# Moving a norm's statistics, transposes and scaled rows ahead of the down projection in the context's first feed-forward

## The reference, cut to what matters

```python
x = first_block(...)                       # ends: x = x + moe(h); return rms_norm(x, final_norm_g)
# second block, layer 0; x_lat is x, x_ctx is the context, 256 tokens x 1024 features each
x_ctx = x_ctx + 0.5 * mc[2] * swiglu(modulate(x_ctx, g, mc[0], mc[1]), w_gate, w_up, w_down)
x_lat = x_lat + 0.5 * m[2]  * swiglu(modulate(x_lat, g, m[0],  m[1]),  w_gate, w_up, w_down)
# modulate(x, g, shift, scale) = x * rsqrt(mean(x*x) + eps) * g * (1 + scale) + shift
# swiglu(x) = (silu(x @ w_gate) * (x @ w_up)) @ w_down, with 2816 hidden features
```

## Time and profile before

| | us |
|---|---|
| median of 3 runs | 2166.23 |
| lowest, highest | 2163.4, 2167.1 |
| the profiled execution, its time | 2169.83 |
| its span, first to last instruction | 2168.0 |

### The profile page before, as it was taken

The page is one execution under the profiler, slowest core; times in us unless marked ns, Lnnn a source line. Parts: engine busy times, 40 slices in busy tenths (PEclk is TensorE's granted clock), DMA queues, the critical chain, the costliest instruction groups (busy, mean ns, idle before and its releaser), DMA issues. The chain is left out here.

```text
span 2168.0 us, 32219 instructions
## 1 busy us (share of the span) xinstructions
PE 2019.4 (93%) x13104; PEld 1613.9 (74%) x13104; DVE 1275.3 (59%) x2026; ACT 882.4 (41%) x1436; POOL 60.5 (3%) x72
## 2 busy tenths in 40 slices
PE   7999999989998889888799999999999999999998
PEld 7897887744445657667788878668888888888887
DVE  5877455462112333334587763577777777877776
ACT  4434354311001222224455443375445554545444
POOL 1000000000000000000100030000001000100000
PEclk9999999989999999999999999999999999999999
DMA  9999984469999999999346453034446464364441
GB/s 363 402 399 359 372 292 155 171 257 422 421 421 414 414 407 410 406 418 331 129 144 233 167 163 117 10 108 165 159 136 230 156 225 155 129 213 166 143 155 40
DMA packets 211166, 540.73 MB, mean 249 GB/s; under 512 B 8894, under 2 KB 105752, under 8 KB 186440
## 3 DMA queue, kind: packets, MB, share of 16 engines
q1 hardware_dynamic: 208264, 531.69, 65.1%
q0 software_dynamic: 2192, 6.57, 1.1%
q10 hardware_dynamic: 560, 0.38, 0.1%
HBM read 537.56 MB, written 1.05 MB: 248 GB/s over the span
## 5 line engine op out<-in xcount | busy, mean ns | idle before, releaser
L1305 PE MATMUL lo<-xs,wp 128*128 128x512 f32 (+1 forms) x3392 | 594.4, 337 | 11.6 <-DVE wp L2678 8.3
L1305 PEld LDWEIGHTS lo<-xs,wp 128*128 128x128 f32 x3392 | 515.8, 190 | 89.7 <-issue 12.8
L987 ACT ACTIVATE wp<-ring 128x1024 fp32r<-128x1024 f32 (+2 forms) x432 | 347.3, 828 | 252.4 <-PE hi L1305 142.0
L2678 DVE TENSOR_TENSOR wp<-ring,wp 128x1024 fp32r<-128x1024 f32 (+2 forms) x432 | 398.8, 943 | 12.0 <-ACT wp L987 11.9
L1305 PE MATMUL hi<-hs,wp 128*128 128x256 f32 (+1 forms) x1842 | 318.8, 334 | 6.3 <-DVE hs L3030 3.2
L1305 PEld LDWEIGHTS hi<-hs,wp 128*128 128x128 f32 x1842 | 276.6, 190 | 45.1 <-DVE hs L3030 3.5
L1305 PE MATMUL lo<-ring,scratch 128*64 128x512 f32 (+1 forms) x1536 | 253.4, 594 | 17.3 <-DMA ring<-in_moe_w_up_dram 9.3
L1305 PEld LDWEIGHTS lo<-ring,scratch 128*64 128x64 f32 (+1 forms) x1536 | 79.7, 123 | 176.7 <-issue 163.7
L2685 DVE TENSOR_TENSOR ring_r<-ring,home 128x1024 fp32r<-128x1024 f32 x52 | 63.0, 1224 | 133.4 <-ACT home L995 133.4
L995 ACT ACTIVATE home<-ring 128x1024 fp32r<-128x1024 f32 x52 | 53.9, 1053 | 189.9 <-DMA ring<-in_ffn_w_down_dram 57.8
L1305 PE MATMUL hi<-xs,home 128*128 128x256 f32 x576 | 108.3, 292 | 14.4 <-DVE ring_r L2685 12.0
(11 more groups left out here) (494 smaller groups left out, 2758.4 us busy)
## 6 DMA issues: line engine op xcount, KB each, us to landing
ring<-in_mod_w_dram SPq DMA_DIRECT2D x72, 1024.0 KB, 15.2
ring<-in_moe_w_gate_dram SPq DMA_DIRECT2D x64, 1024.0 KB, 12.4
ring<-in_moe_w_up_dram SPq DMA_DIRECT2D x64, 1024.0 KB, 15.9
ring<-in_moe_w_down_dram SPq DMA_DIRECT2D x64, 1024.0 KB, 15.4
ring<-in_ffn_w_gate_dram SPq DMA_DIRECT2D x55, 1024.0 KB, 6.0
ring<-in_ffn_w_up_dram SPq DMA_DIRECT2D x55, 1024.0 KB, 8.7
ring<-in_ffn_w_down_dram SPq DMA_DIRECT2D x50, 1024.0 KB, 11.0
ring<-in_w_in_dram SPq DMA_DIRECT2D x20, 1024.0 KB, 13.2
```

Source lines behind the costliest of these rows:

```text
L987: act.activation(wp[:, q % SLOTS, 0, k:k + w.shape[1], :], w, ACT.Copy).then_inc(piece_hi, 2 // len(parts))
L1305: return pe.matmul(dst, lhsT, rhs, start=start, stop=stop, **kw)
L2678: tt(wp[:, q % SLOTS, 1, k:k + w.shape[1], :], w, wp[:, q % SLOTS, 0, k:k + w.shape[1], :].bitcast(F32), ALU.subtract).then_inc(piece_lo, ...
```

## The change: what it does

The order of the steps is changed, and two banks with it; the same values are computed.

- Step 1 moves up on ScalarE: the first half goes behind the rounding of piece 53, the second behind the rounding of hidden tile 17. The roundings of pieces 54 and 55 are now behind both.
- Step 2 moves up on VectorE, now a reciprocal and a product for each half, between the product and the rest of hidden tile 17; the rest of piece 54 comes behind it.
- Step 3 moves from behind up tile 19 to behind up tile 18, and the copy and the square of step 4 from tile 20 to tile 18.
- Step 5 moves from behind up tile 21 to behind up tile 19, into bank hi 0 in place of lo 0. TensorE now waits for rms_std ahead of the down pieces.
- Step 6: the square root goes ahead of the silu of tile 20, the reciprocal to VectorE's tile 20.
- Step 7: chunks 0 to 3 are scaled at VectorE's tile 20, 4 to 7 at tile 21. ScalarE's shift of chunk d comes ahead of the square of the context's chunk d, and VectorE's rest follows one down piece later.

```diff
@@ ScalarE @@
             act.wait_ge(piece_done, EARLY_PIECES - 1)
             round_piece(EARLY_PIECES + 1)
+            act.wait_ge(moe_done, 1)
+            norm_stats(4, x, squares=part(10240, TT, D), halves=(0,))
             early_piece(EARLY_PIECES - 1, False)
+            norm_stats(4, x, squares=part(10240, TT, D), halves=(1,))
...
             round_piece(EARLY_PIECES + 2)
-            act.wait_ge(moe_done, 1)
             round_piece(EARLY_PIECES + 3)
-            norm_stats(4, x, squares=part(10240, TT, D))
             for tile in range(EARLY_TILES, FTILES):
+                if tile == 20:
+                    act.wait_ge(rms_ms, 4)
+                    act.activation(rstd_x, hi[:, 0, 0:T], ACT.Sqrt, bias=eps[:], scale=P / D).then_inc(rms_std, 1)
                 act.wait_ge(piece_done, up_q(0, tile, 0) + 1)
...
                 round_next(up_q(0, tile, 0))
-                if tile == 20:
+                if tile == 18:
                     act.wait_ge(fm_turned, 2)
                     act.activation(xT, hi[:, :, :], ACT.Copy).then_inc(fm_copied, 1)
                 early_hidden(tile)
-                if tile == 20:
+                if tile == 18:
                     act.wait_ge(fm_copied, 2)
                     act.activation(un, xT, ACT.Square).then_inc(rms_sq, 1)
                 round_next(up_q(0, tile, 1))
-            act.wait_ge(rms_ms, 4)
-            act.activation(rstd_x, lo[:, 0, 0:T], ACT.Sqrt, bias=eps[:], scale=P / D).then_inc(rms_std, 1)
             for d in range(KC):
                 round_next(down_q(0, 2, d))
-                squares(0, d, E_FFN[0] + 4 * KC)
                 act.wait_ge(piece_done, up_q(0, FTILES - 1, 1) + 1)
                 norm_hi(1, d, mod[:, 0, 0, 0], xs[:, d, 0], un[:, d])
+                squares(0, d, E_FFN[0] + 4 * KC)
             deviation(0)
@@ TensorE @@
-                if tile == 19:
+                if tile == 18:
+                    pe.wait_ge(h_mul, tile)
                     pe.wait_ge(xg_ready, TT)
...
-            pe.wait_ge(rms_sq, 4)
-            pe.wait_ge(h_mul, FTILES - 1)
-            for c in range(KC):
-                ins = mm(lo[:, 0, 0:T], means[:, 1, :], un[:, c, :], c == 0, c == KC - 1)
-            ins.then_inc(rms_ms, 1)
+                if tile == 19:
+                    pe.wait_ge(rms_sq, 4)
+                    for c in range(KC):
+                        ins = mm(hi[:, 0, 0:T], means[:, 1, :], un[:, c, :], c == 0, c == KC - 1)
+                    ins.then_inc(rms_ms, 1)
+            pe.wait_ge(rms_std, 4)
             for d in range(KC):
@@ VectorE @@
             rest_piece(EARLY_PIECES + 1)
-            early_piece(EARLY_PIECES - 1, False)
+            dve.wait_ge(piece_done, EARLY_PIECES)
+            early_mul(EARLY_TILES - 1, early_bank(EARLY_PIECES - 1)[:, 0])
+            dve.wait_ge(gain_loaded, 16)
+            for t in range(TT):
+                rstd_of(4, t)
+                stt(x[:, t, :], x[:, t, :], rstd[:, t:t + 1], gate_b[:], ALU.mult, ALU.mult).then_inc(xg_ready, 1)
+            rest_piece(EARLY_PIECES + 2)
+            early_lo(EARLY_TILES - 1)
...
-            rest_piece(EARLY_PIECES + 2)
-            dve.wait_ge(gain_loaded, 16)
-            dve.wait_ge(norm_std, TT * 5)
-            link(dve.reciprocal(rstd[:], std[:]))
-            for t in range(TT):
-                stt(x[:, t, :], x[:, t, :], rstd[:, t:t + 1], gate_b[:], ALU.mult, ALU.mult).then_inc(xg_ready, 1)
             for tile in range(EARLY_TILES, FTILES):
                 rest_next(up_q(0, tile, 0))
+                if tile == 20:
+                    dve.wait_ge(rms_std, 4)
+                    link(dve.reciprocal(rstd_x, rstd_x))
+                if tile >= 20:
+                    for c in range(4 * (tile - 20), 4 * (tile - 19)):
+                        scaled(un[:, c], xT, c, mod_scale[:, 1], rstd_x)
                 dve.wait_ge(piece_done, up_q(0, tile, 1) + 1)
...
             for d in range(KC):
-                if d == 1:
-                    dve.wait_ge(rms_std, 4)
-                    link(dve.reciprocal(rstd_x, rstd_x))
                 early_added(down_q(0, 2, d), d, hi[:, d % 4, 0:T])
                 rest_next(down_q(0, 2, d))
                 if d:
-                    scaled(un[:, d - 1], xT, d - 1, mod_scale[:, 1], rstd_x)
-                if d >= 2:
-                    norm_lo(1, d - 2, mod[:, 0, 0, 0])
-            scaled(un[:, KC - 1], xT, KC - 1, mod_scale[:, 1], rstd_x)
-            for c in (KC - 2, KC - 1):
-                norm_lo(1, c, mod[:, 0, 0, 0])
+                    norm_lo(1, d - 1, mod[:, 0, 0, 0])
+            norm_lo(1, KC - 1, mod[:, 0, 0, 0])
```

## The result

| | before | changed |
|---|---|---|
| median of 6 runs each, us | 2166.66 | 2151.34 |
| profiled execution's span, us | 2168.0 | 2154.1 |

The ratio is 0.9927, 95% interval 0.9912 to 0.9941: 15.3 us less at the medians. A second set of runs of the changed kernel gave 0.9928 (0.9909 to 0.9946), median 2148.70. One execution of the kernel before in that second set took 5093 us, more than twice the others, counts as slow and is left out of the ratio. The forecast was 2149.7, in a range from 2146.5 to 2157.0.

The account below looks back on a forecast made before the run. TensorE was taken as the bound, idling before tile 19's second piece and before feed-forward 1. Gains of 4.2, 11.1 and 1.2 us make 16.5, taking the median from 2166.2 to 2149.7 us, range 2146.5 to 2157.

Parts of the forecast that it names:

- Part 1 and 2: Tile 18 to the down pieces: earlier statistics, products, transposes and mean start the downs 4.2 us earlier.
- Part 1: Statistics and x times gain, before tile 19: removes a gap and slow clock costing 4.1 us.
- Rival A: Front doesn't hold: a late product or square loses 2 to 4 of the 4.2 us; chance 0.10.
- Part 3: Square root, reciprocal and scaling at tiles 20 and 21: cost zero, bounds 0 to 1 us.
- Part 4: Down stage of feed-forward 0: the round trip per piece goes, 11.1 us gained, tail included.
- The tail: From the end of the downs to feed-forward 1: taken as 2.9 us, ending with the sums.
- Rival B: Down stage: VectorE or ScalarE becomes the pace at 2.7 us a piece, gain only 11 us; chance 0.05.
- Part 5: Start of feed-forward 1: less half clock, 1.2 us more gain, if TensorE idles under 1 us at a time.
- Rivals C and D: C: half clock lasting from the transposes, about 2167, 0.03 with other slower; D: transfer wait at feed-forward 1, about 2163, 0.04.
- The sum: Whole kernel: 15.3 us to the start of feed-forward 1 plus 1.2 for the clock, 16.5 us.

Follow-up runs that it names:

- experiment 1: Kernel before with only the statistics and the products with the gain (steps 1 and 2) moved up: ratio 0.9982, stretch 60.06 us against 63.90.
- experiment 2: Changed kernel with step 7 undone, so the scaled rows stand late in the down stage again: ratio 0.9986, stretch 58.88 us against 48.61.
- experiment 9: Changed kernel with ScalarE's square first and feed-forward 1's first three pieces one after the other, behind the sums and the dummy: feed-forward 1 starts at 47.97 us.
- Experiments 4 and 5: Kernel before with dummy matmuls in TensorE's idle time: 12 before the sums, 63.88 us stretch; then 13, and two between the sums, 63.56 us.

## Why the prediction was right

**Part 1 and 2, the front.** Predicted 4.2, measured 4.1: the down pieces begin 28.23 us into the stretch (predicted 28.1), before it was 32.34. Part 1 alone gave 3.8 (experiment 1) where 4.1 was worked out. The transposes began at 5.76 us (predicted 5.8). The products ended at 4.9 as worked out, so their spare was the predicted 0.9; the square ended at 11.8 and TensorE came to its sums at 13.3, a spare of 1.5 and not 0.9. Rival A did not happen.

**Part 3.** TensorE had no wait for the root. The two added table loads of ScalarE held nobody up: the silu of tile 20 behind them still waited 0.92 us for TensorE. The 0.1 us that I took for the last hidden tile didn't show.

**Part 4, the down stage.** The 144 matmuls ran without a gap in 17.7 us, and the downs ended at 45.9 (predicted 45.7). From their start to feed-forward 1 it is 20.4 us against 31.6 before, 11.2 less, where 11.1 was worked out. That the order and not VectorE's load was the price is shown by experiment 2. The 3.4 us a turn held for the first turns; the last ones took 3.74. The tail was predicted at 2.9 and is 2.7, and that these agree is in part luck: I let it end with the sums. TensorE waited 0.84 us for GpSimd and not 1 to 1.5, and VectorE's rest of piece 70, which I had not counted, added 0.39 behind the sums (experiment 9). Rival B was at work in small: the last adds of VectorE stand at 1053.25, 1056.00 and 1058.39, 2.4 to 2.75 us apart where TensorE's pieces are 2.16, since beside GpSimd a shift rest takes 0.95 to 1.03 in place of 0.47 and a rest of a piece 1.48 in place of 1.21. No matmul of the downs waited; the rests are ready two pieces ahead, which I take as the reason. The Trainium skill, "SBUF — State Buffer", Who interferes with whom, says that a VectorE instruction with two SBUF inputs contends with a GpSimd instruction that reads SBUF. The rows agree: the shift rest, with two such inputs, doubled, and the add at 1053.25, one of whose inputs is PSUM, stayed at 0.47 though GpSimd was adding from 1053.30 to 1054.04.

**Part 5, the clock.** Predicted 1.2 us, measured 12.69 - 11.34 = 1.35 in the 64 matmuls (1.14 with the second trace's 11.55). Experiments 4 and 5 bear out the cause, with 1.6 as its whole price, and show how thin the condition was: idles of 1.12 and 0.79 brought the half clock, 0.84 did not. Experiment 2, where the 64 took 11.81, shows that the term could have come out 0.9 smaller with the same idle before it.

**Rivals C and D** did not happen: the granted clock is 1.00 in every window of the stretch, and there is no wait for a transfer at the start of feed-forward 1.

The sum was 16.5; by the trace it is 16.65, and the medians say 15.3, with an interval from 12.8 to 19.1 (0.0059 and 0.0088 of 2167). The forecast carried one execution's time over to the median; that this came within 2 us, where single executions of the changed kernel lie 12 us apart, is partly luck, and the stretch is what bears the prediction out.

## What to carry to other kernels

Where two engines trade work piece by piece, count the round trip in their queues' order and not the busy time of either: a 0.4 us row that one engine waits for, behind the other's next piece, cost about 1.3 us each time (10.3 us for eight). Move such a row to where its result lies ready, and see that all that it needs moves with it. When a wait is gone, look for what ends next to it within a few tenths (here the rest of a piece ended 0.39 us behind the sums), because that sets what the next change is worth.

## What the runs showed of the hardware

The stretch repeats to 0.01 us (48.61 and 48.60), so the scatter of the total times comes from elsewhere, and two sources show. Over the twelve traces piece 52 starts anywhere from 1004.85 to 1011.49, without a change ahead of it. And behind it, the feed-forwards of step matmuls (512 and 256 columns in turn) run at one of two paces at the same granted clock of 1.00. The same 128 down matmuls of feed-forward 1 and the 256 up matmuls behind them, before and in experiment 1:

```profile
1124.26 22.77 PE L1305 MATMUL hi<-hs,wp 128*128 128x512 f32 x128
1146.87 45.40 PE L1305 MATMUL lo<-xs,wp 128*128 128x512 f32 x256
```

```profile
1122.41 22.35 PE L1306 MATMUL hi<-hs,wp 128*128 128x512 f32 x128
1144.60 44.54 PE L1306 MATMUL lo<-xs,wp 128*128 128x512 f32 x256
```

That is 22.61 and 22.19 us start to start, 0.353 and 0.347 a pair, and about 3 us over a feed-forward. It changes from one feed-forward to the next and from run to run of one kernel; its cause is open. In every trace the two groups of 128 down matmuls of a feed-forward have the same pace, and of the 48 feed-forwards 1 to 4 of the twelve traces 26 ran at the slower one. The two traces of the changed kernel differ by 11.6 us in their span (2154.1 and 2142.5): piece 52 starts 4.9 us later in the first, and all four feed-forwards run at the slower pace there, two of the four in the second. The traces of before and of the changed kernel in the section on the result both have all four at the slower pace, so the comparison there isn't touched. A difference of 3 us in this kernel is therefore to be read in the stretch and not in the total.
